# The last four output tiles of a transformer block: squares by ScalarE, column sums added in PSUM between the products, eight tiles scaled by VectorE, and one queue for the stores of the first half

## The chip, the cores and the metric

The kernel runs on one core of a Trainium2 chip. The core has five engines that take their instructions in order and meet only at semaphores: TensorE (PE: products into PSUM), VectorE (DVE), ScalarE (ACT), GpSimd (POOL) and SyncE (SP, which here only issues DMAs). The metric is the device time of one execution in microseconds, the median of several runs.

## The reference, cut to what matters

One block over 512 latent tokens of width 2048: a mixer (an S5 scan beside a Hyena convolution), then a SwiGLU feed-forward, a gated residual and a final RMSNorm. Only the end matters here:

```python
x = x + gate_ffn[:, None] * swiglu(modulate(x, norm_ffn[l], shift_ffn, scale_ffn),
                                   w_ffn_in[l], w_ffn_out[l])
...
def rms_norm(x, g):
    xf = x.astype(jnp.float32)
    y = xf * lax.rsqrt(jnp.mean(xf * xf, axis=-1, keepdims=True) + EPS)
    return (y * g.astype(jnp.float32)).astype(x.dtype)

return rms_norm(x, norm_f)
```

The mean of squares runs over all 2048 channels of a token, so no output of a token can be scaled before the last channel of its row is there.

## The kernel before, in words

Everything is held transposed: a tile is 128 channels on the partitions by 512 tokens, and there are 16 tiles (`KT`) of the result, in `xout[:, h, m, :]`. The two halves h of 256 tokens (`CW`) lie apart. Weights and activations are float32, split into a high and a low part; each product is three matmuls (high by high, high by low, low by high).

The down projection (`DOWN`) ends with a chunk (c = 4, six k tiles) for each of the 16 result tiles m. For tiles 0 to 11 PE makes the product for all 512 tokens (L2909 to L2911). VectorE then adds it to the residual (L2244, in `down`), squares the tile (L2248) and adds the square to a running sum in `ct[0]` (L2249, which counts up the semaphore `s_sqo`). Between them ScalarE and VectorE split the weights of the tiles to come (L1330, L2180), and ScalarE multiplies finished tiles by the norm's weight (L1402) for tiles below `N_NORM` = 10.

The last four tiles (`N_LAST`) go in two halves of 256 tokens: all four tiles for half 0, then all four for half 1 (L2971 to L2973: 18 matmuls a tile and half). VectorE follows with `last_tiles(h, i)`: residual (L2345), square (L2348), sum (L2353). For half 0 PE then adds up the 256 columns of `ct[0]` over the partitions (`out_squares`, L2945: two matmuls with one column of ones), placed inside the product of half 1, tile 12, ahead of k = 4. VectorE makes the variance (`variance`, L2364, L2366), ScalarE the root (L1414), VectorE one step of correction (`rstd_column`, L2372 to L2374), and PE spreads the factor over the partitions (`out_rstd`, L2951), into `ps[4]`. After the last product the same comes for half 1, where the square of the last tile is not added by VectorE but is a second pair of matmuls; its factor goes to `ps[5]` for VectorE and to `ps[7]` for ScalarE, which copies it to `rs_out` (L1416), since GpSimd reads SBUF alone.

The scaling of the finished tiles is shared by `N_POOL` = (10, 6): GpSimd multiplies tiles 0 to 9 of half 0 and 0 to 5 of half 1 (L883), VectorE the rest (L2380 for tiles that are already multiplied by the norm's weight, L2382 for the others). The result is stored in pairs of tiles, 256 KB each. ScalarE's queue stores what GpSimd scaled (`store_pairs`, L1409), SP's queue what VectorE scaled (L624). ScalarE issues three pairs of half 0, then waits for the variance and the factor of half 1, and issues the other two pairs of half 0 behind that.

The bank of a plain tile is `d_bank(m)`, and tile 11 is in `ps[6]`:

```python
return ps[(3, 7, 5, 6)[m % 4]]
```

The order of the work is written out by hand on every engine; nothing is scheduled.

## Time and profile before

| what | us |
|---|---|
| median of 3 runs | 2770.4 (2769.35 to 2772.22) |
| the profiled execution, its own time | 2769.97 |
| its span, first to last instruction | 2768.1 |
| PE busy in the span | 2736.1 |
| DVE busy | 2170.2 |
| ACT busy | 1141.1 |
| POOL busy | 383.2 |

In the rows, times are microseconds from the start of the span. A row of the timeline says when an instruction began, how long it took, its engine and line, and in brackets how long the engine had stood idle before it and which instruction ended the wait. Rows of matmuls overlap: each begins when the one before has been fed in, so the time that a matmul costs is the distance between the starts. A float32 matmul that isn't split by hand counts as two records.

### The profile page before, as it was taken

What the parts mean: (1) busy time and instruction counts of PE and PEld (TensorE: products, weight loads), DVE (VectorE), ACT (ScalarE), POOL (GpSimd) and SP (SyncE); (2) the same over time, 40 slices, a digit from 0 to 9 for tenths busy, and PEclk for the clock granted to TensorE, in tenths of its full rate; (3) what the DMA queues carried; (4) which work ended last, traced back from release to release, by engine and by line L of the source; (5) the groups of instructions that cost most, each with busy time, mean ns of one, the idle gap of its engine ahead of it and who ended that gap; (6) DMA issues with size and microseconds to landing.
All of it is one profiled execution on the core that took longest, in us unless ns stands there. A gap on an engine that the chain in (4) does not pass through costs nothing.

```text
span 2768.1 us, 39640 instructions
## 1 busy us (share of the span) xinstructions
PE 2736.1 (99%) x15606; PEld 2315.4 (84%) x15606; DVE 2170.2 (78%) x2974; ACT 1141.1 (41%) x1701; POOL 383.2 (14%) x554
## 2 busy tenths in 40 slices
PE   8999999999999999999999999999999999999998
PEld 3688888888878888888788888888888888998997
DVE  7645776987875676676789999999999887776877
ACT  4332333223443532222245555555555554453542
POOL 2001331002333110011100111111111111000001
PEclk9999999999999999999999999999999999999999
DMA  9936884346666645767644444444443336434432
GB/s 383 331 118 151 197 188 139 123 122 203 223 223 188 228 137 186 243 206 268 227 150 145 154 143 154 145 152 141 153 147 125 125 113 215 142 93 151 138 103 96
DMA packets 144540, 475.27 MB, mean 172 GB/s; under 512 B 24993, under 2 KB 29489, under 8 KB 140130
## 3 DMA queue, kind: packets, MB, share of 16 engines
q1 hardware_dynamic: 85570, 300.90, 33.6%
q0 software_dynamic: 49760, 157.67, 18.0%
q10 hardware_dynamic: 9024, 14.16, 1.4%
q8 instruction: 124, 2.03, 0.3%
q14 instruction: 62, 0.51, 0.1%
HBM read 428.14 MB, written 44.44 MB: 171 GB/s over the span
## 4 chain that ended last, share of the span: by engine, by line
PE 91%; DMA 3%; DVE 3%; ACT 2%; issue 1%; POOL 1%; POOLq 0%; SPq 0%; ACTq 0%; DVEq 0%
PE ps L2881 19%; PE ps L2585 11%; PE ps L2587 11%; PE ps L2586 11%; PE ps L2883 10%; PE ps L2932 3%; PE ps L2931 3%; PE ps L2930 3%; PE ps L2909 2%; PE ps L2910 2%; PE ps L2911 2%; PE ps L2564 2%; PE ps L2602 2%; PE ps L2479 1%; PE ps L2629 1%; PE ps L2458 1%
## 5 line engine op out<-in xcount | busy, mean ns | idle before, releaser
L1433 DVE TENSOR_TENSOR hw_lo<-hw_raw,hw_hi 128x1024 fp32r<-128x1024 f32 x220 | 269.3, 1224 | 316.2 <-ACT hw_hi L890 314.8
L890 ACT ACTIVATE hw_hi<-hw_raw 128x1024 fp32r<-128x1024 f32 x220 | 232.5, 1058 | 674.6 <-DMA hw_raw<-in_w_in 452.2
L2881 PE MATMUL ps<-t_hi_lo,wx_hi 128*128 128x512 f32 x1312 | 412.0, 395 | 0.0
L2126 DVE TENSOR_TENSOR wx_lo<-wx,wx_hi 128x1024 fp32r<-128x1024 f32 x287 | 351.5, 1225 | 41.4 <-ACT wx_hi L1281 36.8
L2585 PE MATMUL ps<-h_hi,hw_hi 128*128 128x512 f32 x896 | 354.0, 395 | 0.0
L2587 PE MATMUL ps<-h_hi,hw_lo 128*128 128x512 f32 x896 | 349.4, 390 | 0.0
L2586 PE MATMUL ps<-h_lo,hw_hi 128*128 128x512 f32 x896 | 348.7, 389 | 0.0
L1281 ACT ACTIVATE wx_hi<-wx 128x1024 fp32r<-128x1024 f32 x287 | 302.1, 1053 | 105.4 <-PE ps L2883 99.4
L2881 PE MATMUL ps<-h_hi_lo,wx_hi 128*128 128x512 f32 x984 | 309.0, 395 | 0.0
L2883 PEld LDWEIGHTS ps<-t_hi_lo,wx_lo 128*128 128x128 f32 x1312 | 246.5, 188 | 58.3
L2883 PE MATMUL ps<-t_hi_lo,wx_lo 128*128 128x256 f32 x1312 | 257.7, 278 | 0.0
L2883 PEld LDWEIGHTS ps<-h_hi_lo,wx_lo 128*128 128x128 f32 x984 | 184.8, 188 | 43.7
L1330 ACT ACTIVATE dw_hi<-dw 128x768 fp32r<-128x768 f32 (+1 forms) x192 | 144.4, 753 | 157.7 <-PE ps L2911 126.7
L2180 DVE TENSOR_TENSOR dw_lo<-dw,dw_hi 128x768 fp32r<-128x768 f32 (+1 forms) x192 | 162.1, 846 | 48.3 <-ACT dw_hi L1330 47.6
L2881 PEld LDWEIGHTS ps<-t_hi_lo,wx_hi 128*128 128x128 f32 x1312 | 199.7, 189 | 0.0
L2585 PEld LDWEIGHTS ps<-h_hi,hw_hi 128*128 128x128 f32 x896 | 168.2, 188 | 36.3 <-issue 2.1
L2587 PEld LDWEIGHTS ps<-h_hi,hw_lo 128*128 128x128 f32 x896 | 168.2, 188 | 35.8
L2586 PEld LDWEIGHTS ps<-h_lo,hw_hi 128*128 128x128 f32 x896 | 168.4, 188 | 33.6
L2883 PE MATMUL ps<-h_hi_lo,wx_lo 128*128 128x256 f32 x984 | 193.3, 278 | 0.0
L2932 PE MATMUL ps<-blk_lo_hi,dw_lo 128*128 128x256 f32 x672 | 190.2, 283 | 0.0
L2931 PE MATMUL ps<-blk_lo_hi,dw_hi 128*128 128x256 f32 x672 | 190.2, 283 | 0.0
L2930 PE MATMUL ps<-blk_lo_hi,dw_hi 128*128 128x256 f32 x672 | 190.2, 283 | 0.0
(433 smaller groups left out, 5709.7 us busy)
## 6 DMA issues: line engine op xcount, KB each, us to landing
wx<-in_w_fi SPq DMA_DIRECT2D x164, 512.0 KB, 3.6
hw_raw<-in_w_in SPq DMA_DIRECT2D x128, 512.0 KB, 5.0
ada1m<-in_w_ar POOLq DMA_DIRECT2D x96, 512.0 KB, 4.7
ada_mix<-in_w_ac SPq DMA_DIRECT2D x16, 2048.0 KB, 10.4
dw<-in_w_fo SPq DMA_DIRECT2D x80, 384.0 KB, 3.1
ada1g<-in_w_ar POOLq DMA_DIRECT2D x32, 512.0 KB, 5.7
hw_raw<-in_w_glu SPq DMA_DIRECT2D x32, 512.0 KB, 4.6
hw_raw<-in_w_out SPq DMA_DIRECT2D x32, 512.0 KB, 4.5
```

The costliest lines, as they stand in the source:

```text
L890: act.activation(hw_hi[slot(n)][:, :], hw_raw[slot(n)][:, :], ACT.Copy).then_inc(w_hi, 1)
L1281: act.activation(wx_hi[o % 4][:, :], wx[x_buffer(p, j)][:, :], ACT.Copy).then_inc(w_hi, 1)
L1433: tt(hw_lo[s][:, :], hw_raw[s][:, :], hw_hi[s][:, :].bitcast(F32), SUB).then_inc(w_lo, 1)
L2126: tt(wx_lo[b][:, :], wx[b][:, :], wx_hi[o % 4][:, :].bitcast(F32), SUB).then_inc(w_lo, 1)
L2585: mm(out, wh(k), xh[:, k0 + k, :], start=first and k == 0, stop=False)
L2586: mm(out, wh(k), xl[:, k0 + k, :], start=False, stop=False)
L2587: ins = mm(out, wl(k), xh[:, k0 + k, :], start=False, stop=last and k == nk - 1)
L2881: mm(out[:, :], wh[:, P * k:P * k + P], both[:, :, k, :], start=opens and k == 0, stop=False, skip_group_check=True)
L2883: ins = mm(out[:, 0:CW], wl[:, P * k:P * k + P], xh[:, k, :], start=False, stop=k == ST - 1, skip_group_check=True)
L2930: mm(out, wh[:, w], b_hi[j][:, k, :], start=opens and k == 0, stop=False, skip_group_check=True)
L2931: mm(out, wh[:, w], b_lo[j][:, k, :], start=False, stop=False, skip_group_check=True)
L2932: ins = mm(out, wl[:, w], b_hi[j][:, k, :], start=False, stop=k == K_S - 1, skip_group_check=True)
```

## The change

ScalarE squares the last four tiles of each half (`last_square`, into eight new tiles `last_sq`), where VectorE did. The squares are no longer added on VectorE: PE adds the columns of `ct[0]` (tiles 0 to 11) and of each of the four squares into one column of PSUM for each 128 tokens, with pairs of matmuls that stand between the products (`first_columns`, `last_columns`). `N_POOL` is (8, 6): GpSimd scales eight tiles of half 0, VectorE eight. SP's queue issues all eight stores of half 0 in the order in which they are expected; ScalarE's queue issues only the three pairs of half 1 that GpSimd scales.

On PE the product of tile 12 for half 0 begins as follows (`dw_hi`, `dw_lo`: the tile's weights; `act`: the activations; a weight load goes with each row). Before:

```order
L2971 MATMUL ps<-act_hi,dw_hi_305 128x256 [waits hw_lo_ready,ffn_out_free]
L2972 MATMUL ps<-act_lo,dw_hi_305 128x256
L2973 MATMUL ps<-act_hi,dw_lo_301 128x256
L2971 MATMUL ps<-act_hi,dw_hi_305 128x256
L2972 MATMUL ps<-act_lo,dw_hi_305 128x256
L2973 MATMUL ps<-act_hi,dw_lo_301 128x256
L2971 MATMUL ps<-act_hi,dw_hi_305 128x256
```

and in the changed kernel, at the same place (`ct_206` is `ct[0]`, and the semaphore in the wait is `s_sqo`):

```order
L2993 MATMUL ps<-act_hi,dw_hi_305 128x256 [waits hw_lo_ready,ffn_out_free]
L2994 MATMUL ps<-act_lo,dw_hi_305 128x256
L2995 MATMUL ps<-act_hi,dw_lo_301 128x256
L2993 MATMUL ps<-act_hi,dw_hi_305 128x256
L2994 MATMUL ps<-act_lo,dw_hi_305 128x256
L2995 MATMUL ps<-act_hi,dw_lo_301 128x256
L2956 MATMUL ps<-ones,ct_206 128x1 [waits xp_or_out_square_ready]
L2956 MATMUL ps<-ones,ct_206 128x1
L2993 MATMUL ps<-act_hi,dw_hi_305 128x256
```

The pair of column sums stands behind k = 1 and waits for the sum of tiles 0 to 11, the last of which VectorE makes after PE's product of tile 11.

On ScalarE the end of the program, behind the last split of weights, was:

```order
L1411 ACT_TABLE_LOAD
L1411 ACTIVATE rstd_tok<-ones 128x4
L1414 ACTIVATE rstd_tok<-rstd_tok 128x2 [waits var_ready]
L1416 ACTIVATE rstd_out<-ps 128x256 [waits rstd_broadcast]
L1409 DMA out<-xout 128x512 [waits decay_abs_or_out_ready_pool] x3
L1414 ACTIVATE rstd_tok<-rstd_tok 128x2 [waits var_ready]
L1416 ACTIVATE rstd_out<-ps 128x256 [waits rstd_broadcast]
L1409 DMA out<-xout 128x512 [waits decay_abs_or_out_ready_pool] x5
```

and is now, from the same place on, less the first three squares:

```order
L1417 ACTIVATE last_square_334<-xout 128x256 [waits ffn_out_free]
L1427 ACTIVATE rstd_tok<-rstd_tok 128x2 [waits var_ready]
L1417 ACTIVATE last_square_335<-xout 128x256 [waits ffn_out_free]
L1422 ACTIVATE rstd_out<-ps 128x256 [waits rstd_broadcast]
L1417 ACTIVATE last_square_336<-xout 128x256 [waits ffn_out_free]
L1417 ACTIVATE last_square_337<-xout 128x256 [waits ffn_out_free]
L1417 ACTIVATE last_square_338<-xout 128x256 [waits ffn_out_free]
L1427 ACTIVATE rstd_tok<-rstd_tok 128x2 [waits var_ready]
L1422 ACTIVATE rstd_out<-ps 128x256 [waits rstd_broadcast]
L1441 DMA out<-xout 128x512 [waits decay_abs_or_out_ready_pool] x3
```

Eight squares came in (334 is tile 15 of half 0, 335 to 338 are half 1), and the five stores of half 0 left this queue.

On VectorE the stretch of half 1, from the end of half 0's factor to the variance of half 1, was:

```order
L2345 SCALAR_TENSOR_TENSOR xout<-ps,mod_x,xout 128x256 [waits hw_used]
L2348 TENSOR_TENSOR ct_208<-xout 128x256 [waits ffn_out_free]
L2353 TENSOR_TENSOR ct_206<-ct_206,ct_208 128x256 [waits dve_chain]
L2382 SCALAR_TENSOR_TENSOR xout<-xout,vecs,ps 128x256 [waits dve_chain]
L2345 SCALAR_TENSOR_TENSOR xout<-ps,mod_x,xout 128x256 [waits hw_used]
```

for tile 13, and the whole stretch is now:

```order
L2366 SCALAR_TENSOR_TENSOR xout<-ps,mod_x,xout 128x256 [waits hw_used] x2
L2392 SCALAR_TENSOR_TENSOR xout<-xout,vecs,ps 128x256 [waits rstd_ready]
L2392 SCALAR_TENSOR_TENSOR xout<-xout,vecs,ps 128x256 x2
L2366 SCALAR_TENSOR_TENSOR xout<-ps,mod_x,xout 128x256 [waits hw_used]
L2392 SCALAR_TENSOR_TENSOR xout<-xout,vecs,ps 128x256 x3
L2366 SCALAR_TENSOR_TENSOR xout<-ps,mod_x,xout 128x256 [waits hw_used]
L2392 SCALAR_TENSOR_TENSOR xout<-xout,vecs,ps 128x256
```

The square and the sum of each tile are gone, and of half 0 VectorE scales two tiles more (8 and 9).

The diff:

```diff
@@ -77,7 +77,7 @@
 D_FIRST = [DOWN.index((c, 0, 0)) for c in range(len(CHUNKS))] + [len(DOWN)]
 N_XC, N_FD = 4, 3 * KT - N_LAST
 D_FREE = (280, 280, 280, 282, 282, 284, 284, 284, 285, 286, 287, 287)
-N_POOL = (10, 6)
+N_POOL = (8, 6)
 N_NORM = max(N_POOL)
 A_TILE = (0, 1, 3, 2)
 PRODUCTS = (0, 4, 5, 1, 3, 6, 2)
@@ -282,6 +282,7 @@
     d_five = at("down_five", 59.5, [P, CW])
     xout = at("xout", 169.75, [P, 2, KT, CW])
     rs_out = at("rstd_out", 59.5, [P, 2, CW])
+    last_sq = [[at(f"last_square{h}{i}", 108 + 4 * h + i, [P, CW]) for i in range(N_LAST)] for h in range(2)]
 
     ps = [nc.alloc_psum_tensor(f"ps{j}", [P, 512], F32) for j in range(8)]
 
@@ -618,11 +619,19 @@
                     for i in ([PRODUCTS.index(j) for j in (3, 0, 2, 1)] if blocked else [i for cc, xx, i in DOWN if (cc, xx) == (c, x)]):
                         down_weights(DOWN.index((c, x, i)))
 
-            for h in range(2):
-                for g in range(N_POOL[h] // 2, 8):
+            def store_pair(h, g):
+
+                if 2 * g < N_POOL[h]:
+                    sp.wait_ge(q_rd, 1 + N_POOL[0] * h + 2 * (g + 1))
+                else:
                     sp.wait_ge(o_rd, (KT - N_POOL[0]) * h + 2 * (g + 1) - N_POOL[h])
-                    sp.dma_start(out_d[h][:, 2 * g:2 * g + 2, :], xout[:, h, 2 * g:2 * g + 2, :]).then_inc(s_out, 16)
-            sp.wait_ge(s_out, 8 * (2 * KT - sum(N_POOL)))
+                sp.dma_start(out_d[h][:, 2 * g:2 * g + 2, :], xout[:, h, 2 * g:2 * g + 2, :]).then_inc(s_out, 16)
+
+            for g in (0, 4, 1, 5, 2, 6, 3, 7):
+                store_pair(0, g)
+            for g in range(N_POOL[1] // 2, 8):
+                store_pair(1, g)
+            sp.wait_ge(s_out, 8 * (2 * KT - N_POOL[1]))
 
         @block.gpsimd
         def _(pool):
@@ -1402,23 +1411,35 @@
                     act.activation(xout[:, :, x - 2, :], xout[:, :, x - 2, :], ACT.Copy,
                                    scale=vecs[:, V_NO + x - 2:V_NO + x - 1]).then_inc(q_norm, 1)
 
-            def store_pairs(h, g0, g1):
-
-                for g in range(g0, g1):
-                    act.wait_ge(q_rd, 1 + N_POOL[0] * h + 2 * (g + 1))
-                    act.dma_start(out_d[h][:, 2 * g:2 * g + 2, :], xout[:, h, 2 * g:2 * g + 2, :]).then_inc(q_out, 16)
-
-            act.activation(rt[:, 6, :], ones[:, 0:4], ACT.Sqrt)
-            for h in range(2):
+            def last_square(h, i):
+
+                act.wait_ge(fd_free, N_FD + 1 + N_LAST * h + i)
+                act.activation(last_sq[h][i][:, :], xout[:, h, KT - N_LAST + i, :], ACT.Square).then_inc(s_sq, 1)
+
+            def last_factor(h):
+
+                act.wait_ge(s_rsb, 2 + 2 * h)
+                act.activation(rs_out[:, h, :], ps[(4, 7)[h]][:, 0:CW], ACT.Copy).then_inc(q_rs, 1)
+
+            def last_sqrt(h):
+
                 act.wait_ge(s_var, 3 + h)
                 act.activation(rt[:, 2, 2 * h:2 * h + 2], rt[:, 1, 2 * h:2 * h + 2], ACT.Sqrt).then_inc(s_sqrt, 1)
-                act.wait_ge(s_rsb, 2 + 2 * h)
-                act.activation(rs_out[:, h, :], ps[(4, 7)[h]][:, 0:CW], ACT.Copy).then_inc(q_rs, 1)
-                if h == 0:
-                    store_pairs(0, 0, 3)
-            store_pairs(0, 3, N_POOL[0] // 2)
-            store_pairs(1, 0, N_POOL[1] // 2)
-            act.wait_ge(q_out, 16 * KT + 8 * sum(N_POOL))
+
+            act.activation(rt[:, 6, :], ones[:, 0:4], ACT.Sqrt)
+            for i in range(N_LAST):
+                last_square(0, i)
+            last_sqrt(0)
+            last_square(1, 0)
+            last_factor(0)
+            for i in range(1, N_LAST):
+                last_square(1, i)
+            last_sqrt(1)
+            last_factor(1)
+            for g in range(N_POOL[1] // 2):
+                act.wait_ge(q_rd, 1 + N_POOL[0] + 2 * (g + 1))
+                act.dma_start(out_d[1][:, 2 * g:2 * g + 2, :], xout[:, 1, 2 * g:2 * g + 2, :]).then_inc(q_out, 16)
+            act.wait_ge(q_out, 16 * KT + 8 * N_POOL[1])
 
         @block.vector
         def _(dve):
@@ -2340,28 +2361,17 @@
 
             def last_tiles(h, i):
 
-                m, half, sq = KT - N_LAST + i, slice(CW * h, CW * h + CW), ct[1 + i % 2]
+                m, half = KT - N_LAST + i, slice(CW * h, CW * h + CW)
                 dve.wait_ge(w_used, N_FFN - 2 * N_LAST + 1 + N_LAST * h + i)
                 stt(xout[:, h, m, :], ps[i][:, half], mod_x[:, 5 * KT + m:5 * KT + m + 1], xout[:, h, m, :],
                     MUL, ADD).then_inc(fd_free, 1)
-                dve.wait_ge(fd_free, N_FD + 1 + N_LAST * h + i)
-                ins = tt(sq[:, half], xout[:, h, m, :], xout[:, h, m, :], MUL)
-                if h and i == N_LAST - 1:
-                    ins.then_inc(s_acc, 1)
-                else:
-                    link(ins)
-                    ins = tt(ct[0][:, half], ct[0][:, half], sq[:, half], ADD)
-                    if i == N_LAST - 1 - h:
-                        ins.then_inc(s_acc, 1)
-                    else:
-                        link(ins)
 
             def variance(h):
 
                 a, b = rt[:, 0, 2 * h:2 * h + 2], rt[:, 1, 2 * h:2 * h + 2]
                 dve.wait_ge(s_ss, 4 + h)
                 for j in range(2):
-                    ins = ts(rt[:, 0, 2 * h + j:2 * h + j + 1], ps[6 + j][:, h:h + 1], 1.0 / D, EPS, MUL, ADD)
+                    ins = ts(rt[:, 0, 2 * h + j:2 * h + j + 1], ps[6 + h][:, j:j + 1], 1.0 / D, EPS, MUL, ADD)
                 link(ins)
                 dve.reciprocal(b, a).then_inc(s_var, 1)
 
@@ -2387,13 +2397,13 @@
             variance(0)
             rstd_column(0)
             last_tiles(1, 0)
+            last_tiles(1, 1)
             dve.wait_ge(q_rs, 3 + 1)
-            scaled_out(0, 10)
-            scaled_out(0, 11)
-            last_tiles(1, 1)
-            scaled_out(0, 12)
+            for k in range(8, 11):
+                scaled_out(0, k)
             last_tiles(1, 2)
-            scaled_out(0, 13)
+            for k in range(11, 14):
+                scaled_out(0, k)
             last_tiles(1, 3)
             scaled_out(0, 14)
             variance(1)
@@ -2938,12 +2948,21 @@
                 elif c < N_XC or x < KT - N_LAST:
                     down_plain(n)
 
-            def out_squares(h, tile, first, last):
-
+            def first_columns(h):
+
+                pe.wait_ge(s_sqo, 2 * KT + KT - N_LAST)
                 for j in range(2):
                     c = slice(CW * h + P * j, CW * h + P * j + P)
-                    ins = mm(ps[6 + j][:, h:h + 1], tile[:, c], ones[:, 0:1], start=first, stop=last)
-                return ins
+                    mm(ps[6 + h][:, j:j + 1], ct[0][:, c], ones[:, 0:1], start=j == 0, stop=False, skip_group_check=True)
+
+            def last_columns(h, i):
+
+                pe.wait_ge(s_sq, 2 * KT + N_LAST * h + i + 1)
+                for j in range(2):
+                    ins = mm(ps[6 + h][:, j:j + 1], last_sq[h][i][:, P * j:P * j + P], ones[:, 0:1], start=False,
+                             stop=i == N_LAST - 1, skip_group_check=True)
+                if i == N_LAST - 1:
+                    ins.then_inc(s_ss, 1)
 
             def out_rstd(h, bank):
 
@@ -2960,10 +2979,13 @@
                     if h == 0:
                         pe.wait_ge(w_lo, N_D + n + 1)
                     for k in range(K_S):
+                        if i == 0 and k == 2:
+                            first_columns(h)
+                        if i and k == 4:
+                            last_columns(h, i - 1)
                         if h == 1 and i == 0 and k == 4:
-                            pe.wait_ge(s_acc, 2)
-                            out_squares(0, ct[0], True, True).then_inc(s_ss, 1)
-                        if h == 1 and i == 1 and k == 3:
+                            last_columns(0, N_LAST - 1)
+                        if h == 1 and i == 1 and k == 5:
                             pe.wait_ge(s_dg, 8)
                             out_rstd(0, ps[4])
                         c, x = slice(P * k, P * k + P), slice(CW * h, CW * h + CW)
@@ -2972,10 +2994,7 @@
                         mm(out, wh[:, c], xl, start=False, stop=False)
                         ins = mm(out, wl[:, c], xh, start=False, stop=k == K_S - 1)
                     ins.then_inc(w_used, 1)
-            pe.wait_ge(s_acc, 3)
-            out_squares(1, ct[0], True, False)
-            pe.wait_ge(s_acc, 4)
-            out_squares(1, ct[2], False, True).then_inc(s_ss, 1)
+            last_columns(1, N_LAST - 1)
             pe.wait_ge(s_dg, 8 + 1)
             out_rstd(1, ps[5])
             out_rstd(1, ps[7])
```

## Rows read from the trace of the kernel before

**Rows 1.** The page, busy time of each engine.

```profile
PE 2736.1 (99%) x15606; PEld 2315.4 (84%) x15606; DVE 2170.2 (78%) x2974; ACT 1141.1 (41%) x1701; POOL 383.2 (14%) x554
```

**Rows 2.** The chain that ended last: start us, us, what.

```profile
2749.63 7.91 POOL xout L883 x10
...
2760.62 3.41 POOL xout L883 x5
```

**Rows 3.** The DMAs' queues from 2745 us on: GB/s in 40 slices of 0.6 us.

```profile
GB/s 0 0 0 27 0 0 0 0 0 0 119 379 355 31 154 287 0 300 376 198 0 0 99 338 0 181 382 382 376 389 382 379 386 372 382 382 365 10 0 0
```

**Rows 4.** The timeline (start us, us, engine, line, op), DMA issues at the end.

```profile
2750.56 13.25 SPq L624 DMA_DIRECT2D out<-xout  x8
...
2759.45 4.96 ACTq L1409 DMA_DIRECT2D out<-xout  x5
```

**Rows 5.** The timeline, PE and DVE, tile 11 to tile 12.

```profile
2736.04 0.28 PE L2971 MATMUL ps<-act_hi,dw_hi 128*128 128x256 f32 x1
...
2736.75 0.28 PE L2971 MATMUL ps<-act_hi,dw_hi 128*128 128x256 f32 x1
...
2737.75 0.69 DVE L2249 TENSOR_TENSOR ct<-ct,ct 128x512 f32<-128x512 f32 x1
```

**Rows 6.** The timeline, PE and DVE, column sums of half 0.

```profile
2744.94 0.48 DVE L2345 SCALAR_TENSOR_TENSOR xout<-ps,mod_x,xout 128x256 f32<-128x256 f32 x1 [0.76 <-PE ps L2973]
...
2745.99 0.28 PE L2973 MATMUL ps<-act_hi,dw_lo 128*128 128x256 f32 x1
2746.39 0.52 PEld L2945 LDWEIGHTS ps<-ones,ct 128*128 128x128 f32 x4 [0.33 <-DVE ct L2353]
...
2747.07 0.28 PE L2972 MATMUL ps<-act_lo,dw_hi 128*128 128x256 f32 x1
```

**Rows 7.** The timeline, PE, an earlier pair of column sums that waits for nothing.

```profile
1437.91 0.50 PE L2805 MATMUL ps<-ones,shift_acc 128*128 128x1 f32 x4
...
1438.60 0.40 PE L2814 MATMUL ps<-y_lo,hw_hi 128*128 128x512 f32 x1
1438.83 0.40 PE L2815 MATMUL ps<-y_hi,hw_lo 128*128 128x512 f32 x1
```

**Rows 8.** The timeline, DVE and PE, half 1 and behind its last product.

```profile
2748.12 0.16 DVE L2374 SCALAR_TENSOR_TENSOR rstd_tok<-rstd_tok 128x2 f32<-128x2 f32 x1
...
2751.42 0.84 DVE L2353 TENSOR_TENSOR ct<-ct,ct 128x256 f32<-128x256 f32 x1
...
2754.22 0.28 PE L2973 MATMUL ps<-act_hi,dw_lo 128*128 128x256 f32 x1
...
2755.04 0.47 DVE L2345 SCALAR_TENSOR_TENSOR xout<-ps,mod_x,xout 128x256 f32<-128x256 f32 x1
...
2756.32 0.61 PE L2945 MATMUL ps<-ones,ct 128*128 128x1 f32 x4 [0.94 <-DVE ct L2348]
...
2756.97 0.22 DVE L2364 TENSOR_SCALAR rstd_tok<-ps 128x1 f32<-128x1 f32 x2 [0.31 <-PE ps L2945]
...
2758.29 1.11 PE L2951 MATMUL ps<-ident,rstd_tok 128*128 128x128 f32 x4 [1.36 <-DVE rstd_tok L2374]
2759.01 1.42 DVE L2380 TENSOR_TENSOR xout<-xout,ps 128x256 f32<-128x256 f32 x4 [0.78 <-PE ps L2951]
```

**Rows 9.** The timeline, ACT and POOL, half 1.

```profile
2759.90 4.14 POOL L883 TENSOR_TENSOR xout<-xout,rstd_out 128x256 f32<-128x256 f32 x6 [2.36 <-ACT rstd_out L1416]
```

**Rows 10.** The line of ScalarE's early squares: ns min/median/max, first and last start.

```profile
L922 ACT ACTIVATE sqr<-c_raw x16: 398/399/417, 39.4 to 49.8; 128x256 f32<-128x256 f32 x16
```

**Rows 11.** Who waited for whom from 30 to 60 us: total, times, longest.

```profile
PE ps L2458 <- DVE mul_mix L1492: 2.3, 1, 2.3
PE ps L2479 <- DVE taps_dif L1476: 1.5, 1, 1.5
```

**Rows 12.** Stretches: us, then PE, PEld, DVE, ACT, POOL busy, PEclk, DMA share, GB/s.

```profile
30.50:44.20 13.70, 9.96 (x48) 3.86 (x46) 8.95 (x12) 3.40 (x11) 5.36 (x4) 0.75 1.01 423
...
2755.00:2760.00 5.00, 2.11 (x12) 1.53 (x11) 3.77 (x14) 0.59 (x2) 2.64 (x5) 0.74 0.42 157
```

## The prediction

> **What bounds the kernel now.** I read the page first: PE is busy 99% of the span [rows 1], so up to the last product only what PE does or waits for counts. The change touches nothing before tile 12, so I went to the last 32 us. The chain that ended last goes from PE to GpSimd's scaling of half 0 and then half 1 [rows 2]; GpSimd's part of half 0 isn't a bound, since it ends at 2757.54 and the factor of half 1 comes to it at 2759.90 [rows 2, 9]. Behind that factor the queues decide: the DMAs run at about 382 GB/s from 2760.2 to 2767.2 without a gap [rows 3]. That is 7.0 us, or ten stores of 262 KB at 0.69 us. Eight are half 1's; the two others are half 0's, which ScalarE could issue only from 2759.45 on, behind the copy of half 1's factor [rows 4]. So three things set the end: when PE ends its last product, the way from there to the factor, and how many stores stand behind it.
>
> **PE: a new wait.** The first pair of column sums stands behind k = 1 of tile 12, half 0. PE begins that tile at 2736.04 and is at k = 2 at 2736.75 [rows 5]. The sum over tiles 0 to 11 ends at 2737.75 + 0.69 = 2738.44 [rows 5]; the pick-up of such an end took 0.05 (2746.34 to 2746.39) [rows 6]. PE isn't reordered, so the products queued behind the pair stand still from 2736.75 to 2738.49: **1.74 us**. VectorE can't be earlier: its three operations on tile 11 follow PE's product of tile 11. Everything behind on PE waits with it, and VectorE and ScalarE wait for PE.
>
> **PE: the pairs.** Nine pairs of column sums stand ahead of the end of the last product: four in half 0 (the running sum; squares of tiles 12 to 14) and five in half 1 (the running sum, the square of tile 15 of half 0, squares of tiles 12 to 14). Before there was one. What a pair costs can be read twice. One that PE waited for began at 2746.39, and the second product behind it at 2747.07; less a product's 0.12 that is 0.55 [rows 6]. One that waited for nothing began at 1437.91, its second product behind at 1438.60; less the spacing of these wider products (1438.60 to 1438.83, 0.23) that is 0.46 [rows 7]. I take 0.55 for the first pair, 0.46 for eight: **4.23 us**. The ends are 9 x 0.46 = 4.1 and 9 x 0.55 = 5.0.
>
> The row shows four records in a pair at 0.12 each. The Trainium skill ("TensorE: Matmul & The Clock Gate", Back-to-back issue gap) gives a matmul of up to 64 columns about 25 ns; by that alone a pair would cost 0.1 us and the nine 0.9. But the same page (LDWEIGHTS) makes the weight load of 128 columns last 128/1.2 GHz = 107 ns, four of which are 0.43 us. The trace agrees with the second.
>
> Are the squares there in time? ScalarE takes 0.40 for one [rows 10], VectorE's residual 0.48 [rows 6]. For tile 12 of half 0 PE ends at about 2740.5, the square is ready some 1.3 us later (0.27 drain, 0.48, 0.40 and the hand-overs), and PE asks for it 1.44 us after its end (four k of 0.36). That is just enough. Only the square of tile 12, half 1 is late: VectorE is then in half 0's factor. The pair that gives half 0's variance now begins at about 2750.24 (2746.40 before), the correction ends 1.88 us after its start (2746.40 to 2748.28 [rows 8]), so at 2752.12; residual and square end at about 2753.1, PE asks at 2752.86. A wait of about 0.2 and a blocked pair: **0.26 us**.
>
> What leaves: the one pair, 0.55, and its wait for VectorE's sum, 2746.11 to 2746.40: **0.84 us** [rows 6]. PE's last product therefore moves by 1.74 + 4.23 + 0.26 - 0.84 = **+5.39 us**.
>
> **From the last product to the factor.** Before: last product begun 2754.22, VectorE's variance 2756.97, 2.75 us [rows 8]. In it VectorE was late: the residual began 0.82 after the last product's start. It was 0.39 for the last tile of half 0 (2744.55, twelve products of 0.12 ahead of 2745.99, to 2744.94) [rows 6]. VectorE lost this to half 1's squares and sums, of which one took 0.84 beside GpSimd [rows 8]. Now: 0.39 + residual 0.48 + 0.04 + square 0.40 + 0.05 + pair and hand-over 0.65 (2756.32 to 2756.97) = 2.0. **-0.75 us**. The rest to the factor stays as it is.
>
> That one operation took 0.84 where its twin, with GpSimd idle, took 0.42. The Trainium skill ("SBUF — State Buffer", Who interferes with whom) says that a VectorE operation with both inputs in SBUF and GpSimd block each other. All that VectorE now does beside GpSimd reads one input from PSUM. By the page the delay goes wholly, as in my term; if it were a chance delay, about 0.4 of the 0.75 would stay.
>
> So the factor of half 1 comes 5.39 - 0.75 = **4.64 us** later, for VectorE at 2763.65, for GpSimd at 2764.54. The factor of half 0 comes about 5.2 later too (2749.63 to 2754.8 for GpSimd), which costs nothing: eight tiles at the 0.79 of the ten before [rows 2] end at 2761.1. For VectorE two more tiles of under 0.5 each lie beside PE's products.
>
> **The stores.** Half 0 now leaves by SP as it is ready; its last pair (tiles 14, 15) follows the second variance, at about 2762.5, and is through before half 1's first. Eight stores are left, 8 x 0.69 = 5.5 us instead of 6.9. The first pair is ready at 2763.65 + 0.71 = 2764.36, and flows 0.85 after its issue (2750.56 to about 2751.4 [rows 3, 4]), at 2765.2. VectorE makes a pair in 0.7 (four tiles in 1.42 [rows 8]), a little more for tiles that aren't yet multiplied by the norm's weight, so the first ones leave small gaps (0.3 together): the end of the data is 2771.0, against 2767.2. GpSimd's last tile, at 2759.90 + 4.14 + 4.64 = 2768.7, plus 0.85 and 0.69, would end at 2770.2 and doesn't decide. The stores give back **-0.85 us** of the 4.64; the ends are -1.4 (two stores whole) and 0.
>
> **Sum.** +1.74 + 4.23 + 0.26 - 0.84 - 0.75 - 0.85 = **+3.8 us**. The profiled execution took 2769.97 (0.4 under the median), so it would take 2773.8, and the median goes from 2770.4 to **2774.2 us**. A measurement of this kernel can tell about 0.2%, 5.5 us, from no change: +3.8 lies within.
>
> Costed at nothing: ScalarE's two multiplications by the norm's weight that go (they lie beside PE's products), the longer list of SP, the load of ScalarE's tables. The changed order has one load ahead of the squares and the root, as before, and none between them.
>
> **Rivals.**
>
> 1. *The clock falls in the new wait* (25%). PE stands still for 1.74 us in the middle of its products. At the start of the program, after waits of 2.3 and 1.5 us [rows 11], the granted clock was 0.75 on the mean over 13.7 us, so for about 6.9 us it was at 1.2 GHz instead of 2.4; at the end it fell once PE's work had become thin, 0.74 over 2755 to 2760 [rows 12]. Against it: PE was busy on both sides of my wait as it wasn't at the start. If it falls once, for half of that 6.9 us, a product of 256 columns costs 0.21 instead of 0.12 for 3.4 us, a loss of 1.5: +5.3, **2775.7**. With pairs at 0.55 and nothing from the stores it is +6.9, **2777.3**, slower by more than 0.2%. [...]
>
> 2. *The stores give nothing back* (14%). If the receipt of the last store, and not the queue, sets the end, the 4.64 pass through: +4.6, **2775.0**.
>
> 3. *The relief wins: not slower* (9%). If PE hides the pairs beside its weight loads and the wait for the sum doesn't show, what is left is -0.84 - 0.75 - 0.85 = -2.4, **2768.0**. It decides from where wait and pairs together cost under 2.4 us. Against it stand both prices of a pair, 0.46 at the lowest, nine of which are 4.1 by themselves.
>
> **How the numbers follow.** The forecast itself has 52%, with its own range 2772.6 to 2775.6 (pairs 4.1 to 5.0, stores -1.4 to 0). The range that should hold 8 in 10 reaches down a third of the way to rival 3 and up over rival 1's first figure: 2771.2 to 2777.0. Slower by over 0.2% (above 2775.9): nearly half of rival 1, a fifth of rival 2, some of the forecast's upper edge and of the spread of runs, 0.21. Faster by over 0.2% (under 2764.9) needs more than rival 3 gives, 0.03. Within 0.2%: 0.76.
>
> **What would show it.** In the changed kernel's timeline: a gap on PE of 1.7 us ahead of the first pair (L2956), released by VectorE's sum L2270; L2962 and L2956 costing 0.46 to 0.55 each between starts of products; the last product begun near 2759.6; ScalarE's last square 0.4 us and the variance 2.0 after that product's start; GpSimd's second half from 2764.5; DMAs without a gap from 2765.2 to about 2771. Wrong would be: no gap at the first pair (then -1.7), granted clock under 1.00 between 2738 and 2755 (rival 1), PE waiting for squares in several tiles, or data that end less than 0.3 us before GpSimd's last store could.

## The result, and the profile after

Over 15 runs the changed kernel took 2777.39 us (2772.84 to 2779.96) and the kernel before 2772.37 (2768.42 to 2774.74). The ratio is 1.0017 (95% interval 1.0010 to 1.0024): 4.7 us slower, with an interval from 2.8 to 6.7 us (the medians lie 5.0 apart). The forecast was +3.8 us and 2774.2. The forecast difference lies in the interval; the measured time lies 0.4 us over the top of the stated range, 2777.0, so the prediction missed. Of the 35 executions of the kernel before in the last round of experiments, two were in a slow state (3337 and 4544 us, at granted clocks of 0.82 and 0.56), and they are left out of every comparison.

The profiled execution took 2775.43 (span 2773.5). Its PE begins tile 12 of half 0 at 2737.94, and before it was 2736.04 [rows 5]. So 1.9 of the 5.4 us between the two spans lie ahead of everything that was changed; the rest, 3.5, is read from there on. The timeline around the first pair of column sums (start us, us, engine, line):

```profile
2737.94 0.28 PE L2993 MATMUL ps<-act_hi,dw_hi 128*128 128x256 f32 x1
...
2738.53 0.28 PE L2995 MATMUL ps<-act_hi,dw_lo 128*128 128x256 f32 x1
...
2739.65 0.69 DVE L2270 TENSOR_TENSOR ct<-ct,ct 128x512 f32<-128x512 f32 x1
2740.40 0.61 PE L2956 MATMUL ps<-ones,ct 128*128 128x1 f32 x4 [1.59 <-DVE ct L2270]
...
2741.07 0.28 PE L2994 MATMUL ps<-act_lo,dw_hi 128*128 128x256 f32 x1
```

PE could have gone on at 2738.65 (0.12 behind the row of 2738.53) and does at 2740.40: 1.75 us, released by VectorE's sum. The pair, to the second product less 0.12, costs 0.55, as the waiting pair did in [rows 6]. A pair that finds its square ready:

```profile
2743.81 0.50 PE L2962 MATMUL ps<-ones,last_square 128*128 128x1 f32 x4
...
2744.38 0.28 PE L2994 MATMUL ps<-act_lo,dw_hi 128*128 128x256 f32 x1
```

costs 0.45 (0.46 in [rows 7]). The one square that is late, that of tile 12 in half 1:

```profile
2754.53 0.28 PE L2995 MATMUL ps<-act_hi,dw_lo 128*128 128x256 f32 x1
2754.74 0.61 PE L2962 MATMUL ps<-ones,last_square 128*128 128x1 f32 x4
...
2755.41 0.28 PE L2994 MATMUL ps<-act_lo,dw_hi 128*128 128x256 f32 x1
```

PE's pair begins 0.09 behind its place (2754.53 and 0.12) and costs 0.55. The timeline behind the last product, which answers to [rows 8, 9]:

```profile
2761.30 0.28 PE L2995 MATMUL ps<-act_hi,dw_lo 128*128 128x256 f32 x1
...
2761.62 0.48 DVE L2366 SCALAR_TENSOR_TENSOR xout<-ps,mod_x,xout 128x256 f32<-128x256 f32 x1 [0.95 <-PE ps L2995]
...
2762.14 0.42 ACT L1417 ACTIVATE last_square<-xout 128x256 f32<-128x256 f32 x1 [2.18 <-DVE xout L2366]
...
2762.60 0.61 PE L2962 MATMUL ps<-ones,last_square 128*128 128x1 f32 x4 [1.02 <-ACT last_square L1417]
...
2763.25 0.23 DVE L2374 TENSOR_SCALAR rstd_tok<-ps 128x1 f32<-128x1 f32 x2 [0.76 <-PE ps L2962]
...
2764.57 1.11 PE L2970 MATMUL ps<-ident,rstd_tok 128*128 128x128 f32 x4 [1.36 <-DVE rstd_tok L2384]
...
2766.18 4.15 POOL L892 TENSOR_TENSOR xout<-xout,rstd_out 128x256 f32<-128x256 f32 x6 [4.07 <-ACT rstd_out L1422]
```

VectorE is no longer late: the residual starts 0.32 behind the last product (0.82 before), and the variance 1.95 instead of 2.75. The DMAs from 2745 us on, 40 slices of 0.75 us (GB/s), against [rows 3]:

```profile
GB/s 0 0 0 0 0 0 0 22 0 0 0 0 0 0 0 0 0 0 202 385 377 371 380 371 361 0 175 175 0 298 328 333 380 377 385 366 331 0 0 11
```

Half 0's stores are over before half 1's begin: a zero, the last pair of half 0 by itself, a zero, and then eight stores. Before, two stores of half 0 stood among them. Up to the last product the clock did not fall in this execution (stretches: us, then PE, PEld, DVE, ACT, POOL busy, PEclk, DMA share, GB/s):

```profile
2740.50:2748.00 7.50, 7.50 (x64) 7.50 (x65) 2.03 (x4) 0.83 (x2) 0.00 (x0) 1.00 0.00 0
2748.00:2762.00 14.00, 13.58 (x114) 13.24 (x113) 5.70 (x18) 2.67 (x7) 5.47 (x8) 1.00 0.23 86
```

All profiles of this study, read in the same way (us). *Tile 12* is the start of PE's first product of tile 12, half 0; *last* from there to the start of the last product; *var* from there to VectorE's variance of half 1; *GpSimd* from there to GpSimd's start on half 1; *end* from there to the end of the span; *sum* is last to end added; *clock* says where the granted clock was under 1.00 between 2700 us and the last product. The kernels other than before and changed are those of the experiments below.

| kernel | tile 12 | last | var | GpSimd | end | sum | clock |
|---|---|---|---|---|---|---|---|
| before | 2736.04 | 18.18 | 2.75 | 2.93 | 8.20 | 32.06 | |
| null_before | 2737.48 | 18.18 | 2.75 | 2.47 | 8.22 | 31.62 | |
| changed | 2737.94 | 23.36 | 1.95 | 2.93 | 7.32 | 35.56 | |
| null_after | 2737.56 | 23.37 | 1.96 | 2.93 | 7.38 | 35.64 | |
| late_first | 2738.47 | 21.89 | 1.95 | 2.93 | 7.36 | 34.13 | |
| early_first | 2740.81 | 22.65 | 1.95 | 2.93 | 7.36 | 34.89 | fell |
| filled_wait | 2736.09 | 23.37 | 1.95 | 2.47 | 7.42 | 35.21 | |
| twice_pairs | 2738.05 | 26.05 | 1.95 | 2.90 | 7.35 | 38.25 | |
| after_act_stores | 2739.76 | 24.84 | 1.95 | 2.93 | 9.62 | 39.34 | fell |
| dve_squares | 2737.49 | 25.29 | 1.96 | 2.93 | 7.33 | 37.51 | fell |
| before_sp_stores | 2736.36 | 18.18 | 2.75 | 2.47 | 7.44 | 30.84 | |
| dve_sums | 2739.39 | 18.34 | 1.95 | 3.20 | 7.22 | 30.71 | |
| sums_tidy | 2737.21 | 17.82 | 1.94 | 2.92 | 7.71 | 30.39 | |
| sums_warm | 2738.48 | 17.81 | 1.96 | 2.94 | 7.71 | 30.42 | |

The row of early_first can't be set beside the others as it stands: there the wait and the pair stand ahead of the first product, so its tile 12 begins behind them. Counted from the pair's place, 2737.82, its *last* is 25.6 and its *sum* 37.9.

Between the first two profiles the change took +5.18, -0.80, 0 and -0.88: +3.50. Between the second profiles of the same two kernels it is 35.64 less 31.62, +4.02, since *GpSimd* differs there by 0.46; the first experiment says why.

### The profile page after: what moved, and what is told of

It is laid out like the page before. It is cut to its first block, busy times and chain, and to the rows that moved or that the text cites. A ratio compares the mean times of both kernels' runs of the same rounds, so it can differ in the third digit from the quotient of the medians.

```text
span 2773.5 us, 39683 instructions
## 1 busy us (share of the span) xinstructions
PE 2738.2 (99%) x15634; PEld 2318.2 (84%) x15634; DVE 2163.8 (78%) x2961; ACT 1144.0 (41%) x1707; POOL 382.0 (14%) x552
## 4 chain that ended last, share of the span: by engine, by line
PE 92%; DMA 3%; DVE 2%; ACT 2%; issue 1%; POOL 0%; POOLq 0%; ACTq 0%; SPq 0%; DVEq 0%
PE ps L2891 19%; PE ps L2595 11%; PE ps L2597 11%; PE ps L2596 11%; PE ps L2893 10%; PE ps L2942 3%; PE ps L2941 3%; PE ps L2940 3%; PE ps L2919 2%; PE ps L2920 2%; PE ps L2921 2%; PE ps L2574 2%; PE ps L2612 2%; PE ps L2489 1%; DMA hw_raw<-in_w_in 1%; PE ps L2639 1%
```

## The experiments

The theory was that the terms of the prediction add up behind tile 12; the rivals were that part of the loss lies ahead of it, that pairs or stores hide, and that the clock falls in the wait.

### The same kernels again (null_before, null_after)

No edit.

> The kernel before, unchanged, once more: how far does a profile of the same program move? Theory A (the part ahead of tile 12 varies from run to run, by the loads at the start): the product of tile 12, half 0 begins anywhere within some 2 us of 2736.0, while the distance from there to the end of the span stays 32.1 us within 0.3. Theory B (the 1.9 us by which that product began later in the changed kernel belongs to the change): it begins at 2736.0 within 0.3. Time against the kernel before: ratio 1.000 within its interval by both.

> The changed kernel, unchanged, once more, on the same chip. Theory A: tile 12 begins anywhere within some 2 us of 2737, no later on the mean than in the kernel before; from there to the end of the span it takes 35.6 us within 0.3, 3.5 more than before. Theory B: tile 12 begins at 2737.9 again, and the time is 5 us over the kernel before in every comparison. Ratio by A about 1.0013, by B about 1.0019.

Ratios 1.0004 (0.9995 to 1.0013) and 1.0020 (1.0010 to 1.0029). Tile 12 of the unchanged program began 1.4 us later than in its first profile, so theory B falls in its first form: a start 1.9 us later needs no change to the program. By the times alone the two theories can't be told apart: A put the second ratio at 1.0013 and B at 1.0019, 1.0020 was measured, and the interval holds both. The part behind tile 12 repeats within 0.1, but for one thing, which puts null_before 0.2 outside what A allowed. In null_before the spreading of half 1's factor ran at the full clock:

```profile
2759.73 0.65 PE L2951 MATMUL ps<-ident,rstd_tok 128*128 128x128 f32 x4 [1.36 <-DVE rstd_tok L2374]
```

0.65 us against 1.11 in [rows 8], and the whole end 0.44 earlier. The table shows it under *GpSimd*: 2.47 where these transposes ran at the full clock, 2.90 to 2.93 where they did not (in the last three rows VectorE adds to it). They ran at the lower clock in one of the three profiles of kernels whose PE is as before (the third is before_sp_stores), and in all seven of the changed kernel and its variants other than filled_wait. The prediction took this way as unchanged. By these few profiles it may add up to 0.3 us (two thirds of 0.46) to the change; why the clock falls there in one execution and not in another isn't shown.

### The first pair two steps into tile 13 (late_first)

```diff
-                        if i == 0 and k == 2:
+                        if i == 1 - h and k == 2:
                             first_columns(h)
```

(The first pair of half 0 moves from tile 12 to tile 13. That of half 1 stays where it was, in tile 12.)

> The changed kernel with the first pair of column sums of half 0 two k steps into tile 13 instead of tile 12. If the wait for VectorE's sum costs what the gap shows: no gap at that pair (VectorE's sum is ready 0.5 us before PE comes to it), the pair costs 0.46 instead of 0.55, tile 12's begin to the last product is 21.5 us instead of 23.4, and tile 12's begin to the end of the span is 33.8 instead of 35.6. If the gap is slack that would come back elsewhere (at the pairs that wait for ScalarE's squares), the distance to the end stays over 35 us.

Ratio 1.0009 (1.0001 to 1.0018). The sum fell by 1.43, so the wait was on the path; I had expected 1.8. The rest went into a new wait, for the square of tile 12 (the timeline of PE, VectorE and ScalarE):

```profile
2740.91 0.96 DVE L2201 TENSOR_TENSOR dw_lo<-dw,dw_hi 128x768 fp32r<-128x768 f32 x1
2741.79 0.48 DVE L2366 SCALAR_TENSOR_TENSOR xout<-ps,mod_x,xout 128x256 f32<-128x256 f32 x1
...
2742.30 0.42 ACT L1417 ACTIVATE last_square<-xout 128x256 f32<-128x256 f32 x1 [1.26 <-DVE xout L2366]
...
2742.39 0.28 PE L2995 MATMUL ps<-act_hi,dw_lo 128*128 128x256 f32 x1
2742.77 0.61 PE L2962 MATMUL ps<-ones,last_square 128*128 128x1 f32 x4
```

VectorE splits the last weights until tile 12's residual is overdue; PE, no longer held up, now stands 0.26 us (2742.51 to 2742.77) at that pair, which costs 0.55.

### Six pairs more (twice_pairs)

```diff
-                for j in range(2):
+                for j in (0, 1, 2, 3) if i < N_LAST - 1 else (0, 1):
```

with the columns of the square taken by `j % 2`, so PE works through each pair of tiles 12 to 14 a second time. The second pair goes into two further columns of the bank (`j` of 2 and 3), which nobody reads, and not into the same ones as the text below has it.

> The changed kernel with each pair of column sums of the squares of tiles 12 to 14 of both halves made twice (the second adds the same sums again, so that the variance is of other data). Six pairs more stand ahead of the last product's end. If a pair is paid on PE: 6 x 0.46 = 2.8 us more from tile 12's begin to the last product (23.4 to 26.1), and as much in the end. If pairs hide beside PE's weight loads: under 0.5 us more.

Ratio 1.0020 (1.0010 to 1.0030). *Last* grew by 2.69, 0.45 a pair, as much as the pairs that it had: pairs don't hide, and with the wait of late_first rival 3 falls. The timing alone would not have shown this, since the ratio is that of the changed kernel.

### The stores (before_sp_stores, after_act_stores)

The kernel before, its five GpSimd pairs of half 0 moved to SP:

```diff
+            for g in (5, 0, 1, 2, 6, 3, 4, 7):
+                store_pair(0, g)
```

> The kernel before with only the stores changed: all eight pairs of half 0 on SP's queue in the order in which they are ready, ScalarE's queue with the three of half 1. If the queue of stores sets the end: DMAs begin to flow without a gap about 0.5 us later than before and have eight stores instead of ten behind the factor; the end of the span comes 0.85 us earlier (at most 1.4): 31.2 us from tile 12's begin instead of 32.1. If GpSimd's last tile and the receipt of its store set the end: no change, 32.1.

The changed kernel, its four GpSimd pairs of half 0 on ScalarE's queue behind the second factor:

```diff
-            for g in (0, 4, 1, 5, 2, 6, 3, 7):
+            for g in (4, 5, 6, 7):
                 store_pair(0, g)
```

> The changed kernel with GpSimd's four pairs of half 0 stored by ScalarE's queue, behind the copy of half 1's factor (it can't come earlier there without holding up the squares), SP with VectorE's nine. Twelve stores instead of eight then stand behind the factor. If the queue sets the end: 4 x 0.69 = 2.8 us more, less up to 1.2 us in which the queue would otherwise wait for its first pair and small gaps: tile 12's begin to the end of the span 35.6 + 1.6 to 2.3 = 37.2 to 37.9. If the last scaled tile sets the end: 35.6 still.

Ratios 1.0001 (0.9992 to 1.0011) and 1.0027 (1.0015 to 1.0039). *End* went from 8.20 to 7.44 (-0.76; 0.85 was expected) and from 7.32 to 9.62 (+2.3; 1.6 to 2.3). Both have the sign of the queue theory and about its size; rival 2 falls. In the second the DMAs ran without a gap from 2770 us to their end, as long as twelve stores take. The row begins at 2755 us, in slices of 0.6:

```profile
GB/s 0 0 0 0 0 0 0 0 0 0 0 218 219 0 0 345 314 215 0 0 0 0 369 68 41 389 386 359 389 382 372 375 379 382 372 382 389 379 266 0
```

The same profile held something else. *Last* is 24.84 instead of 23.36, though nothing ahead of the last product was edited. Stretches of it (us, then PE, PEld, DVE, ACT, POOL busy, PEclk, DMA share, GB/s):

```profile
2742.00:2744.00 2.00, 1.78 (x13) 1.78 (x14) 1.13 (x2) 0.32 (x2) 0.00 (x0) 0.84 0.00 0
2744.00:2746.00 2.00, 2.00 (x11) 2.00 (x11) 0.48 (x1) 0.39 (x1) 0.00 (x0) 0.50 0.00 0
2746.00:2748.00 2.00, 2.00 (x16) 2.00 (x16) 0.00 (x0) 0.02 (x1) 0.00 (x0) 0.81 0.00 0
2748.00:2750.00 2.00, 2.00 (x20) 2.00 (x19) 0.48 (x1) 0.42 (x1) 0.00 (x0) 1.00 0.00 0
```

After the wait (it ended at 2742.22) the granted clock fell to 0.50, 1.2 GHz, and came back: 1.48 us lost, the 1.5 of rival 1. Nothing else of PE's part differs from the changed kernel's, and without this loss its *sum* would be 37.9.

### A longer wait, and a filled one (early_first, filled_wait)

```diff
-                        if i == 0 and k == 2:
+                        if i == 0 and k == (2 if h else 0):
```

> The changed kernel with the first pair of column sums two k steps earlier, ahead of the first product of tile 12. PE's wait for VectorE's sum grows by 0.72 to 2.3 us. Without a fall of the clock tile 12's last product ends as before it, since the sum sets when PE goes on: the two products' k steps come behind the pair, so the last product is 23.4 + 0.7 = 24.1 us behind the first place of the pair. If the granted clock falls behind such a wait (rival 1 of the prediction; it fell in two of six profiles of kernels with the 1.6 us wait), 25.6 and a stretch below 1.00 between 2740 and 2750.

```diff
+                        if h == 0 and i == 0 and k == 2:
+                            for _ in range(14):
+                                mm(ps[4][:, 0:CW], wh[:, 0:P], a_hi[:, 0, 0:CW], start=True, stop=True)
                         if i == 0 and k == 2:
```

> The changed kernel with 14 products of 256 columns, whose result nobody reads, in the place of PE's wait for VectorE's sum (14 x 0.12 = 1.68 us; the wait was 1.59 by the engine's idle time). Tile 12's begin to the last product stays 23.4 within 0.15, and the granted clock stays 1.00 throughout. If the fall of the clock in part of the executions is what the changed kernel's times have beyond the 3.5 us of its profile, its ratio comes to about 1.0013 to 1.0016 instead of 1.0017 to 1.0020.

(The first of these texts says two of six profiles; it was two of five.) In early_first the clock fell again. PE behind the wait:

```profile
2740.37 0.58 PE L2956 MATMUL ps<-ones,ct 128*128 128x1 f32 x4 [2.39 <-DVE ct L2270]
...
2741.84 0.37 PE L2995 MATMUL ps<-act_hi,dw_lo 128*128 128x256 f32 x1
2742.01 0.42 PE L2993 MATMUL ps<-act_hi,dw_hi 128*128 128x256 f32 x1
2742.23 0.41 PE L2994 MATMUL ps<-act_lo,dw_hi 128*128 128x256 f32 x1
2742.44 0.41 PE L2995 MATMUL ps<-act_hi,dw_lo 128*128 128x256 f32 x1
```

Products stand 0.21 apart from 2742.01 on, and 0.12 before. The pair's place was 2737.82 (0.23 behind the last wide product, at 2737.59) and the last product began 22.65 behind 2740.81, at 2763.46: 25.6 us, as expected with the fall. With the wait filled, *last* is 23.37, the same as with it, and the clock stayed at 1.00 over both stretches:

```profile
2736.00:2745.00 9.00, 9.00 (x77) 8.85 (x75) 4.06 (x6) 3.17 (x5) 0.00 (x0) 1.00 0.00 0
2745.00:2759.00 14.00, 14.00 (x119) 13.87 (x119) 5.55 (x17) 2.67 (x7) 4.31 (x7) 1.00 0.15 55
```

Ratios 1.0016 (1.0007 to 1.0025) and 1.0014 (1.0005 to 1.0023): the times can't tell the two from the changed kernel or from each other. Over all profiles, the clock fell in two of the five with the 1.6 us wait, in the one with 2.4 us, and in none of the eight without a wait in that place. One filled profile that stayed up is no proof that filling prevents it, since three of five stayed up unfilled.

### Squares on VectorE, sums on PE (dve_squares)

```diff
+                dve.wait_ge(fd_free, N_FD + 1 + N_LAST * h + i)
+                tt(last_sq[h][i][:, :], xout[:, h, m, :], xout[:, h, m, :], MUL).then_inc(s_sq, 1)
```

in `last_tiles`, and `last_square` no longer called on ScalarE.

> The changed kernel with the squares on VectorE again (one operation a tile behind the residual), column sums on PE as changed. Tells what ScalarE's part is worth by itself. If VectorE's squares with two SBUF inputs are slowed beside GpSimd: the squares of half 1 take 0.6 to 0.85 instead of 0.42 wherever GpSimd is at work, the last one not (GpSimd has ended half 0 by then); from the last product to the variance 1.95 us as now, since VectorE is no longer late. So by my reading the -0.75 came from the sums that left VectorE's queue, and ScalarE's part is worth nothing at the end; half 0's pairs wait for nothing either. Rival: the square on VectorE delays the residual or the last square: 0.3 us or more later.

Ratio 1.0020 (1.0010 to 1.0029). *Var* is 1.96, as foreseen: the gain at the end comes from what left VectorE's queue, not from ScalarE's being the one to square. But *last* is 25.29. The clock fell here as well, which cost about 1.5 us, and in half 1 a square was late (a stretch behind the wait, then VectorE's timeline):

```profile
2742.00:2744.00 2.00, 2.00 (x11) 2.00 (x11) 0.91 (x2) 0.00 (x0) 0.00 (x0) 0.50 0.00 0
```

```profile
2760.67 0.92 DVE L2364 TENSOR_TENSOR last_square<-xout 128x256 f32<-128x256 f32 x1
...
2763.61 0.42 DVE L2364 TENSOR_TENSOR last_square<-xout 128x256 f32<-128x256 f32 x1
```

0.92 us beside GpSimd, 0.42 once GpSimd is done; PE's pair began at 2761.64, 0.26 behind its place (2761.26 and 0.12). Wait and dearer pair make 0.36, and 25.29 less 23.36 and 1.5 is 0.4. So ScalarE's part is worth some 0.4 us after all: my expectation had regard only to the last square.

### ScalarE squares, VectorE sums, one pair between the products (dve_sums, sums_tidy, sums_warm)

The kernel before with `before_sp_stores`' stores, `last_square` on ScalarE, and on VectorE behind each residual only the sum:

```diff
+                dve.wait_ge(s_sq, 2 * KT + N_LAST * h + i + 1)
+                ins = tt(ct[0][:, half], ct[0][:, half], last_sq[h][i][:, :], ADD)
```

PE's one pair of half 0 stands ahead of k = 5 and not k = 4. The two later versions change what their texts say.

> The kernel before with ScalarE's squares, VectorE adding them to the running sum as before, PE with only one pair of column sums between the products (half 0, one k later than before) and two behind the last product, GpSimd still scaling ten tiles of half 0, and all stores of half 0 on SP's queue. It has the two gains of the change without its price on PE. By my sum: last product 0.3 earlier than before (the wait for VectorE's sum gone), 0.75 less from there to the variance, 0.85 to 1.4 less in the stores: tile 12's begin to the end of the span 32.1 - 1.9 = 30.2 us, within 0.4; ratio about 0.9993. Rival: VectorE's additions beside GpSimd are slowed as before and VectorE is still late for the last tile; then 31.0 or more.

> The version with ScalarE's squares and VectorE's sums once more, with three places mended that its trace showed: VectorE makes half 0's factor ahead of the residual of tile 12, half 1, PE takes that factor in one k later, and VectorE scales its last tiles of half 0 around half 1's variance and not ahead of it. From tile 12's begin: last product 17.9 (18.34 there), variance 1.95 later, GpSimd's second half 2.93 after that (3.20 there; 2.47 where the clock stays up), end 7.2 later: 30.0 us (29.5 with the clock up) against 32.1 before. Ratio 0.9991. Rival: the residual of tile 12, now behind the factor, makes a sum late; then 30.5.

> That version, with 16 products on PE whose result nobody reads, in the three waits behind the last product (three, three and ten of 0.12 us). Theory (clock): the granted clock stays at 1.00 up to the spreading of half 1's factor; that takes 0.46 us less for the copy to ScalarE than at the lower clock (2.93 to 2.47, as in the profile of the repeated kernel before), in every execution and not in some: 29.5 us from tile 12's begin. Rival: the products hold PE when the squares or the factor come, and the factor is later by up to 0.3.

All three had a ratio of 0.9994 (0.9985 to 1.0003): not shown to be faster than before, and by the intervals faster than the changed kernel. From tile 12 on they take 30.7, 30.4 and 30.4 us against 31.6 to 32.1 before and 35.6 changed. Most of that gain is the stores': before_sp_stores, with only these changed, takes 30.8 (with the full clock in the spreading). I had expected 30.2, 30.0 (29.5 with the clock up) and 29.5. *Var* came in all three, and *last* in the two later ones (17.8; 18.34 in dve_sums). *End* was 7.71 in these two and not 7.2, which wasn't followed further. The clock stayed up for the spreading in sums_warm, but in sums_tidy as well, without the products that nobody reads, so the two don't show that these keep it up. What a clock that stays up gives was lost on VectorE (three rows of sums_warm, then one of sums_tidy, then the same multiplication in the changed kernel):

```profile
2758.59 0.46 DVE L2399 SCALAR_TENSOR_TENSOR xout<-xout,vecs,ps 128x256 f32<-128x256 f32 x1
2758.97 0.15 DVE L2389 SCALAR_TENSOR_TENSOR rstd_tok<-rstd_tok 128x2 f32<-128x2 f32 x1
2759.16 0.64 DVE L2390 TENSOR_TENSOR rstd_tok<-rstd_tok 128x2 f32<-128x2 f32 x1
```

```profile
2757.88 0.61 DVE L2390 TENSOR_TENSOR rstd_tok<-rstd_tok 128x2 f32<-128x2 f32 x1
```

```profile
2764.16 0.16 DVE L2383 TENSOR_TENSOR rstd_tok<-rstd_tok 128x2 f32<-128x2 f32 x1
```

A tiny multiplication took 0.64 and 0.61 where it takes 0.16, since GpSimd's ten tiles of half 0 now run beside it: it ended at 2759.80 and 2758.49, and GpSimd's run at 2759.78 and 2758.47. In the changed kernel GpSimd had eight and was done.

## Why the prediction missed

Its terms behind tile 12 were right, one by one, in mechanism and nearly in size. The wait: 1.74 said, 1.75 measured. Nine pairs: 4.23 said; 0.55 for the first and 0.45 for each other measured, 4.15. The late square and its pair: 0.26 said, 0.18 measured (PE's pair of tile 12, half 1 waited 0.09). The last product: +5.39 said, +5.18 measured. From there to the variance: -0.75 said, -0.80 measured. The stores: -0.85 said, -0.88 measured. Together +3.8 said, +3.50 measured in the first pair of profiles and +4.02 in the second. GpSimd's start on half 1 was said for 2764.54; less the 1.9 us by which this execution was late, it was 2764.28.

Two steps failed, and neither is a term of the change.

The first made the miss: the base in "the median goes from 2770.4 to 2774.2", to which the range of "How the numbers follow" then gave no room of its own. The 2770.4 rested on three runs. The kernel before has medians of 2772.37, 2771.84, 2772.16 and 2772.53 us over 15 to 35 runs; single runs spread by 6 to 7 us within 15 of either kernel, and by up to 12.8 us within 35 of the kernel before. In the profiles PE reached one same product in the middle of the program (the shift sums, [rows 7]: 1437.9) anywhere from 1437.5 to 1440.6, and the rest of the way to tile 12 varied by 1.3 us. With the base of the 15 runs, +3.8 gives 2776.2, inside the stated range. Of the 2.8 us that the range had above the forecast, a base 2.0 us off used up most. The forecast's own range, 2772.6 to 2775.6, doesn't follow from the prices in its brackets either: pairs of 4.1 to 5.0 and stores of -1.4 to 0 give 2773.5 to 2775.8.

Second, rival 1 was set beside the forecast, as if one of the two were to happen. It happens in some executions of one and the same list of PE (that of after_act_stores is the changed kernel's). The fall costs 1.5 us, as said; at two in five it would add 0.6 to a mean, 4.1 us in all, inside the interval of 2.8 to 6.7. That share comes from five profiles of related kernels and is only a rough one. With up to 0.3 us for the lower clock in the spreading it would be 4.4. Whether what is beyond that, 0.3 us to the 4.7 here and 1.1 to the 5.5 of null_after's ratio, is anything at all isn't settled: tile 12 began on the mean at 2737.9 in the eight profiles of kernels made from the changed one (for early_first the pair's place) and at 2737.5 in the six made from the one before, with over 3 us of spread in each.

*Var* fell by the whole lateness of VectorE, and by as much in dve_squares, where VectorE still makes the squares: the relief is the work that left its queue. The Trainium skill ("SBUF — State Buffer", Who interferes with whom) says that a VectorE instruction with two SBUF inputs contends with a GpSimd instruction that reads SBUF. The traces agree: such operations took 0.92 and 0.64 beside GpSimd instead of 0.42 and 0.16.

## What to carry to other kernels

A pair of float32 column sums is four records on PE and cost 0.45 us here, though each product has a single column; where PE is the bound, let an engine with slack add the tiles and make one pair for all (*last* was 17.8 so, and 23.4 with the pairs and the wait). A wait put into PE's stream costs time each time (1.4 of its 1.75 us came back when it was taken out) and, in some executions, 1.5 us more in clock behind it. Where the effect is a few microseconds in thousands, predict the difference, and give the absolute time a range that also holds what is unknown of the base; and read such an effect from distances within the profile, counted from the last point that the change can't have touched.

## What was not expected of the hardware

- The same program fell to the lower clock in one profile and not in another at the end, 0.65 and 1.11 us for the same four transposes (null_before and before); with one and the same wait of 1.6 us it fell in two profiles of five.
- The way to one and the same product at 1440 us varied by 3.1 us over 14 profiles; what it depends on was not followed.
